# Last down-projection chunk of a decoder step by token thirds, with the final norm of a third beside the next third and two thirds scaled on GpSimd

## The chip, the core and the metric

The kernel runs on one core of a Trainium2 chip. The metric is the device time of one execution in microseconds (us), lower is better. Five engines work side by side, each through its own queue of instructions in order: TensorE (PE), VectorE (DVE), ScalarE (ACT), GpSimd (POOL) and SyncE (SP), which here only issues DMAs. They wait for one another through semaphores.

## The reference, cut to what matters

One step of a decoder layer for 1024 prompt tokens and 8 sample tokens, 1032 in all, in a model of width 1024. Only its end matters here: the feed-forward block (ConvFFN, 2816 hidden features) and the final norm.

```python
def conv_ffn(hn, buf, w_up, conv_w, conv_b, w_down):
    ...
    a, gt = jnp.split(conv, 2, axis=-1)
    return (a * jax.nn.silu(gt)) @ w_down, full[:, T:]
...
        x = x + f
...
    y = rmsnorm(x, P['norm_final'])

def rmsnorm(x, g):
    r = lax.rsqrt(jnp.mean(x * x, axis=-1, keepdims=True) + EPS)
    return (x * r) * g
```

## The kernel before

Activations lie with the 128 features of a tile on the partitions and the 1032 tokens along a row. There are KT = 8 feature tiles; XR[:, m, :] is the residual stream x of tile m. A product of a weight tile with 1032 tokens runs as NTG = 3 matmuls of TG = 344 tokens, each into its own PSUM bank. Every float32 product is made of three float32r products, of the rounded operands and the remainders: WH with HH, WH with HL, WL with HH (L256, L257, L259). ScalarE rounds a weight slab to WH (L245, `act_hi`), VectorE subtracts to get WL (L250, `dve_lo`), and both use two slots in turn. `acc(slot)` is a group of three banks: banks 0 to 2 and 3 to 5. TensorE fills a group and raises `acc_ready`; the engine that empties it raises `acc_free[slot]`.

The hidden features come in 11 chunks of 256. A loop makes a chunk of the up projection (4 groups) and then the down projection of the chunk before (8 groups, one for each m, k = 2 weight tiles each, so 18 matmuls a group). VectorE adds each group to XR (L2400). After the loop `down(0, N_SLABS - 2, ...)` does the last chunk's down projection. It needs the last two weight slabs: the four m of slab N_SLABS - 2 first, then the four of slab N_SLABS - 1. For each m, VectorE adds the group to XR (L2429), ScalarE squares the new XR tile into TMP (L390), and VectorE adds the squares to SS (L399; SS is the tile GT).

Then comes the final norm, once for all 1032 tokens. `pe_norm` sums SS over the partitions by 9 matmuls with a column of ones (L415), so that a token stands on a partition. ScalarE takes the root (L428). VectorE inverts it (L444) and spreads it onto diagonals in SS (L446, L448; `dve_norm_diag`). TensorE multiplies a matrix of ones with SS (L421), which brings the scale of each token to all partitions, and ScalarE copies it to RB (L432). VectorE scales the eight tiles of XR by RB and by the gain in one scalar_tensor_tensor each (L2434, in place), and SyncE stores each tile once it is there (L2440, `sp_final`). GpSimd does nothing in this stretch; its last instruction is the DMA of `up_state` (L2252).

For a norm in the middle of the kernel (`pe_entry`) the same steps run in between other matmuls: L1931 is the sum over partitions, L1937 the spreading. Early in the kernel GpSimd prepares tables, with tensor_tensor in lines L660 and L741 and L780, and tensor_scalar with a per-partition scalar from SBUF in L711 to L713.

Of the kernel before, what the change touches and what calls it, by code (L numbers as in the profile page):

```python
# [30 lines left out]
ACT = mybir.ActivationFunctionType  # L31
# [3 lines left out]
D = 1024  # L35
# [99 lines left out]
def program(nc, I, O):  # L135
    ctx = ExitStack()
    with ctx:
        def sem(name):
            return ctx.enter_context(nc.semaphore(name))
# [246 lines left out]
        def act_square(act, done, count, tile, slot, width):  # L386

            if done is not None:
                act.wait_ge(norm_dve, done)
            nc.scalar.activation(TMP[:, slot, 0:width], tile, ACT.Square).then_inc(sq_ready, 1)  # L390
# [1801 lines left out]
        def dve_cross(dve, st):  # L2192
# [18 lines left out]
            for t in range(8):  # L2211
                if t == MID + 2:
# [29 lines left out]
        ffn_in, u_slots, f_conv, f_silu, f_mul, f_hi, f_lo = (sem("ffn_in"), sem("u_slots"), sem("f_conv"),  # L2242
                                                               sem("f_silu"), sem("f_mul"), sem("f_hi"), sem("f_lo"))
        y_ready, y_stored, f_stored = sem("y_ready"), sem("y_stored"), sem("f_stored")

        def pool_ffn(pool):
            pool.wait_ge(acc_ready, G_CO + KT)
            pool.dma_start(FW[:], I["ffn_w"]).then_inc(ffn_in, 16)
            pool.dma_start(FB[:], I["ffn_buf"]).then_inc(ffn_in, 16)
            pool.dma_start(O["buf1"], I["buf1"]).then_inc(f_stored, 16)  # L2250
            pool.wait_ge(u_slots, 2 * NF + 2)
            pool.dma_start(O["up_state"], UPS[:]).then_inc(f_stored, 16)  # L2252
            pool.wait_ge(f_stored, 32)
            pool.wait_ge(mem_kv_out, 32)
            pool.wait_ge(s5_stored, 16)
            pool.wait_ge(ml_out, 160)
            pool.wait_ge(gl_out, 64)

        def pe_ffn(pe):
            def up(i, n, g, per_n, per_g, first=0):  # L2260
                for k in range(first, 4):
                    pe.wait_ge(w_lo, i * per_n + (n + k + 1))
                    pe.wait_ge(acc_free[(g + k) % 2], i * (per_g // 2) + (g + k) // 2)
                    split_product(pe, banks((g + k) % 2), (n + k) % 2, next_hi_cols, next_lo_cols, 0, KT).then_inc(acc_ready, 1)

            def down(i, n, g, buf, h_need, per_n, per_g, per_h):
                pe.wait_ge(f_lo, i * per_h + h_need)
                for s in range(2):
                    pe.wait_ge(w_lo, i * per_n + (n + s + 1))
                    for m in range(4):  # L2270
                        gg = g + 4 * s + m
                        pe.wait_ge(acc_free[gg % 2], i * (per_g // 2) + gg // 2)
                        split_product(pe, banks(gg % 2), (n + s) % 2,
                                      lambda k, t: HH[:, buf, k, t * TG:(t + 1) * TG],
                                      lambda k, t: HL[:, buf, k, t * TG:(t + 1) * TG],
                                      m, 2, 4).then_inc(acc_ready, 1)

            pe_entry(pe, SL_FFN, G_FFN, 3, 5)
            up(0, SL_FFN, G_FFN, 0, 0, 2)
            with pe.Fori(0, (NF // 2 - 1) // 2) as i:  # L2280
                for c in range(2):
                    n, g = SL_FFN + 4 + 6 * c, G_FFN + 4 + 12 * c
                    up(i, n, g, 12, 24)
                    down(i, n + 4, g + 4, c, 2 * c + 2, 12, 24, 4)
            down(0, N_SLABS - 2, G_FFN + 124, 0, NF, 0, 0, 0)

            pe_norm(pe, 4, N, G_FFN + 132)

        def act_ffn(act, st):
            act_entry(act, 3)  # L2290
# [27 lines left out]
            with act.Fori(0, (NF // 2 - 1) // 2) as i:  # L2318
                for c in range(2):
                    n, g = SL_FFN + 4 + 6 * c, G_FFN + 4 + 12 * c  # L2320
                    up(i, n, g, 4 + 4 * c, (c + 1) % 2, 12, 24, 8, False)
                    down(i, n + 4, g + 4, 4 + 4 * c, (c + 1) % 2, 12, 24, 8)
            for m in range(KT):
                g = G_FFN + 124 + m
                act.wait_ge(acc_free[g % 2], g // 2 + 1)
                act_square(act, 36 + m - 1, None, XR[:, m, :], m % 2, N)
            act_norm(act, 4, 6, N)

        def dve_ffn(dve, st):
            L = st.link  # L2330
# [86 lines left out]
            with dve.Fori(0, (NF // 2 - 1) // 2) as i:  # L2417
# [3 lines left out]
                    up(i, n, g, 4 + 4 * c, 2 + 2 * c, (c + 1) % 2, 12, 24, 8, False)  # L2421
                    down(i, n + 4, g + 4, 4 + 4 * c, 2 + 2 * c, (c + 1) % 2, 12, 24, 8)
                st.leave((NF // 2 - 1) // 2)
            L(nc.vector.memset(SS[:, :], 0.0))
            for m in range(KT):
                g = G_FFN + 124 + m
                dve.wait_ge(acc_ready, g + 1)
                x = XR[:, m, :]
                nc.vector.tensor_tensor(t3(x), t3(x), acc(g % 2), AD).then_inc(acc_free[g % 2], 1)  # L2429
                dve_sum(dve, KT * 4 + m, False, m % 2, N, 36 + m)  # L2430

            dve_norm_diag(dve, st, 4, N)
            for kt in range(KT):
                nc.vector.scalar_tensor_tensor(out=XR[:, kt, :], in0=XR[:, kt, :], scalar=GAIN[:, 4, kt:kt + 1],  # L2434
                                               in1=RB[:, :], op0=M, op1=M).then_inc(y_ready, 1)

        def sp_final(sp):
            for kt in range(KT):
                sp.wait_ge(y_ready, kt + 1)
                sp.dma_start(O["y"][:, kt, :], XR[:, kt, :]).then_inc(y_stored, 16)  # L2440
            sp.wait_ge(y_stored, 16 * KT)

        @block.sync
        def _(sp):
# [4 lines left out]
        def _(pool):  # L2449
# [9 lines left out]
            pool_gla(pool)  # L2459
            pool_gates(pool)  # L2460
            pool_cross(pool)
            pool_ffn(pool)

        @block.scalar
        def _(act):
# [215 lines left out]
```

## Time and profile before

| | us |
|---|---|
| median of 3 runs | 2369.13 (2362.12 to 2372.32) |
| profiled execution, its own time | 2369.92 |
| its span, first to last instruction | 2367.3 |
| PE busy in the span | 2260.8 |
| DVE busy | 1145.2 |
| ACT busy | 597.0 |
| POOL busy | 281.7 |

The span is what the views of the profile show; the execution's own time is 2.6 us longer. Busy times are sums over an engine's instructions. Line numbers such as L2429 are those of the code printed above. In the names of the profile `ps` is PSUM, and `out<-in` stands for the tile written and the tiles read.

### The profile page before, as it was taken

What the parts mean: (1) busy time and instruction counts of PE and PEld (TensorE: products, weight loads), DVE (VectorE), ACT (ScalarE), POOL (GpSimd) and SP (SyncE); (2) the same over time, 40 slices, a digit from 0 to 9 for tenths busy, and PEclk for the clock granted to TensorE, in tenths of its full rate; (3) what the DMA queues carried; (4) which work ended last, traced back from release to release, by engine and by line L of the source; (5) the groups of instructions that cost most, each with busy time, mean ns of one, the idle gap of its engine ahead of it and who ended that gap; (6) DMA issues with size and microseconds to landing.
All of it is one profiled execution on the core that took longest, in us unless ns stands there. A gap on an engine that the chain in (4) does not pass through costs nothing.

```text
span 2367.3 us, 34371 instructions
## 1 busy us (share of the span) xinstructions
PE 2260.8 (95%) x14712; PEld 2177.6 (92%) x14712; DVE 1145.2 (48%) x1264; ACT 597.0 (25%) x740; POOL 281.7 (12%) x436
## 2 busy tenths in 40 slices
PE   5799989999999999999999999999999999999995
PEld 5699978888989999999999998999999999999995
DVE  4716533334444344323654222437566655556665
ACT  4422233222322222233332124222111111111112
POOL 5989700000000000000000000000000000000000
PEclk9899999999989999999999999999999999999998
DMA  6311123121322222224322143111111111111111
GB/s 234 107 45 48 51 92 109 55 72 73 126 101 82 79 77 88 105 81 191 134 99 88 45 169 143 36 46 54 45 46 48 51 46 45 46 45 46 54 40 72
DMA packets 45221, 190.36 MB, mean 80 GB/s; under 512 B 5136, under 2 KB 5200, under 8 KB 41488
## 3 DMA queue, kind: packets, MB, share of 16 engines
q1 hardware_dynamic: 32112, 117.13, 14.4%
q0 software_dynamic: 11104, 54.41, 6.1%
q10 hardware_dynamic: 1872, 16.83, 1.8%
q8 instruction: 111, 1.82, 0.3%
q14 instruction: 22, 0.18, 0.0%
HBM read 152.59 MB, written 35.93 MB: 80 GB/s over the span
## 4 chain that ended last, share of the span: by engine, by line
PE 88%; issue 4%; DVE 3%; ACT 2%; POOL 1%; DMA 1%; DVEq 0%; ACTq 0%; POOLq 0%
PE ps L256 24%; PE ps L257 24%; PE ps L259 24%; PE ps L1715 1%; PE ps L1006 1%; PE ps L2043 1%; PE ps L2067 1%; DVE GT L399 1%; PE ps L371 1%; PE ps L372 1%; PE ps L374 1%; PE ps L2077 1%; POOL W L660 1%; PE ps L1691 0%; DVE WL L250 0%
## 5 line engine op out<-in xcount | busy, mean ns | idle before, releaser
L256 PE MATMUL ps<-XH,WH 128*128 128x344 f32 x1656 | 536.5, 327 | 8.5 <-DVE WL L250 6.0
L257 PE MATMUL ps<-XL,WH 128*128 128x344 f32 x1512 | 481.4, 322 | 0.0
L256 PE MATMUL ps<-XN,WH 128*128 128x344 f32 x1248 | 399.2, 322 | 4.3 <-issue 4.1
L257 PE MATMUL ps<-XN,WH 128*128 128x344 f32 x1248 | 397.2, 322 | 0.0
L250 DVE TENSOR_TENSOR WL<-WRAW,WH 128x1024 fp32r<-128x1024 f32 x175 | 220.3, 1260 | 309.3 <-ACT WH L245 308.2
L259 PE MATMUL ps<-XH,WL 128*128 128x344 f32 x1656 | 353.2, 322 | 0.0
L256 PEld LDWEIGHTS ps<-XH,WH 128*128 128x128 f32 x1656 | 314.8, 190 | 19.7 <-issue 14.4
L245 ACT ACTIVATE WH<-WRAW 128x1024 fp32r<-128x1024 f32 x175 | 184.3, 1054 | 534.6 <-PE ps L259 522.5
L257 PEld LDWEIGHTS ps<-XL,WH 128*128 128x128 f32 x1512 | 286.8, 190 | 0.2
L259 PEld LDWEIGHTS ps<-XH,WL 128*128 128x128 f32 x1656 | 279.4, 190 | 0.0
L259 PE MATMUL ps<-XN,WL 128*128 128x344 f32 x1248 | 264.3, 320 | 0.0
L256 PEld LDWEIGHTS ps<-XN,WH 128*128 128x128 f32 x1248 | 235.0, 188 | 6.4 <-issue 6.2
L257 PEld LDWEIGHTS ps<-XN,WH 128*128 128x128 f32 x1248 | 234.9, 188 | 0.5 <-issue 0.5
L259 PEld LDWEIGHTS ps<-XN,WL 128*128 128x128 f32 x1248 | 209.3, 188 | 0.0
L256 PE MATMUL ps<-HH,WH 128*128 128x344 f32 x528 | 167.7, 321 | 1.6 <-DVE XR L2429 1.6
L257 PE MATMUL ps<-HL,WH 128*128 128x344 f32 x528 | 167.1, 320 | 0.0
L2382 DVE TENSOR_TENSOR UB<-ps,RB 128x1032 f32<-128x1032 f32 x44 | 54.3, 1233 | 179.2 <-PE ps L259 173.5
L2400 DVE TENSOR_TENSOR XR<-XR,ps 128x1032 f32<-128x1032 f32 x80 | 98.2, 1228 | 34.5 <-PE ps L259 34.5
L311 ACT ACTIVATE STAGE<-ps 128x1032 f32<-128x1032 f32 x40 | 41.2, 1030 | 290.1 <-PE ps L259 290.1
L259 PE MATMUL ps<-HH,WL 128*128 128x344 f32 x528 | 111.9, 320 | 0.0
L256 PEld LDWEIGHTS ps<-HH,WH 128*128 128x128 f32 x528 | 99.5, 188 | 2.8 <-DVE XR L2429 2.0
L257 PEld LDWEIGHTS ps<-HL,WH 128*128 128x128 f32 x528 | 99.4, 188 | 0.0
(512 smaller groups left out, 3165.9 us busy)
## 6 DMA issues: line engine op xcount, KB each, us to landing
WRAW<-in_wslabs SPq DMA_DIRECT2D x175, 512.0 KB, 3.5
scratch_spill<-STAGE SPq DMA_DIRECT2D x40, 516.0 KB, 2.6
ZS<-scratch_spill POOLq DMA_DIRECT2D x24, 516.0 KB, 5.5
XIN<-in_xT POOLq DMA_DIRECT2D x1, 4128.0 KB, 18.4
XR<-in_xT ACTq DMA_DIRECT2D x2, 2064.0 KB, 8.7
out_y<-XR SPq DMA_DIRECT2D x8, 516.0 KB, 3.0
CACHES<-in_ck ACTq DMA_DIRECT2D x4, 1024.0 KB, 14.2
CACHES<-in_cv ACTq DMA_DIRECT2D x4, 1024.0 KB, 15.6
```

What stands on the lines that cost most here:

```text
L245: nc.scalar.activation(WH[:, slot], WRAW[:, slot], ACT.Copy).then_inc(w_hi, 1)
L250: nc.vector.tensor_tensor(WL[:, slot], WRAW[:, slot], WH[:, slot].bitcast(F32), ALU.subtract).then_inc(w_lo, 1)
L256: pe.matmul(out[t], WH[:, slot, w, :], xh(k, t), start=(k == 0), stop=False)
L257: pe.matmul(out[t], WH[:, slot, w, :], xl(k, t), start=False, stop=False)
L259: last = pe.matmul(out[t], WL[:, slot, w, :], xh(k, t), start=False, stop=(k == nk - 1))
L311: nc.scalar.activation(t3(staged(g)), acc(0), ACT.Copy, scale=FILL_SCALE[g]).then_inc(fl_free, 1)
L371: pe.matmul(out[t], WH[:, slot, k, :], xh_cols(k, t), start=(k == 0), stop=False)
L372: pe.matmul(out[t], WH[:, slot, k, :], xl(k, t), start=False, stop=False)
L374: last = pe.matmul(out[t], WL[:, slot, k, :], xh_cols(k, t), start=False, stop=(k == KT - 1))
L399: nc.vector.tensor_tensor(SS[:, 0:width], SS[:, 0:width], TMP[:, slot, 0:width], ALU.add).then_inc(norm_dve, 1)
L2382: nc.vector.tensor_tensor(t3(UB[:, k % 2, 2:N + 2]), acc((g + k) % 2), t3(RB[:, :]), M).then_inc(acc_free[(g + k) % 2], 1)
L2400: nc.vector.tensor_tensor(t3(x), t3(x), acc(gg % 2), AD).then_inc(acc_free[gg % 2], 1)
```

## The change

The last chunk's down projection runs over thirds of the tokens on the outside and over m on the inside. A group is then one m of one third: six matmuls into one bank, `ps[:, i % 6, 0:TG]`, with i = 8t + m from 0 to 23. Six banks are used in turn. TensorE waits for both last slabs (`w_lo >= N_SLABS`) before the first group.

VectorE adds a group to a third of XR (`add`), ScalarE squares it into one of four small tiles SQ, VectorE adds it to the third of SS (`total`; for m = 0 a copy, so the memset goes). The norm of third t - 1 runs between the groups of third t: the sums over partitions after its group m = 3 (`pe_end_columns`, 3 columns), root and diagonals (`act_end_root`, `dve_end_diag`), the spreading after group m = 5 (`pe_end_spread`), and the copy to RB (`act_end_rows`). The last third's norm follows its last group.

GpSimd scales the first two thirds (`pool_end`): for each m a tensor_scalar with the gain and then a tensor_tensor with RB, in place on 344 tokens, the second waiting for the first; 32 instructions. VectorE scales the last third, one instruction for each m. SyncE stores six pieces in place of eight, each of four tiles m of one third, in the order of the thirds; rows of 344 tokens (1376 bytes) in place of 1032 tokens.

The diff, without the parts that only pass arguments:

```diff
@@ -2242,14 +2242,26 @@
         ffn_in, u_slots, f_conv, f_silu, f_mul, f_hi, f_lo = (sem("ffn_in"), sem("u_slots"), sem("f_conv"),
                                                                sem("f_silu"), sem("f_mul"), sem("f_hi"), sem("f_lo"))
         y_ready, y_stored, f_stored = sem("y_ready"), sem("y_stored"), sem("f_stored")
-
-        def pool_ffn(pool):
+        end_added, G_END = acc_free[0], G_FFN + 124
+        ADDED = (G_END + 1) // 2
+        SQ = at("SQ", [128, 4, TG], O_TMP)
+
+        def third(t):
+
+            return slice(t * TG, t * TG + TG)
+
+        def end_bank(i):
+
+            return ps[:, i % 6, 0:TG]
+
+        def pool_ffn(pool, st):
             pool.wait_ge(acc_ready, G_CO + KT)
             pool.dma_start(FW[:], I["ffn_w"]).then_inc(ffn_in, 16)
             pool.dma_start(FB[:], I["ffn_buf"]).then_inc(ffn_in, 16)
             pool.dma_start(O["buf1"], I["buf1"]).then_inc(f_stored, 16)
             pool.wait_ge(u_slots, 2 * NF + 2)
             pool.dma_start(O["up_state"], UPS[:]).then_inc(f_stored, 16)
+            pool_end(pool, st)
             pool.wait_ge(f_stored, 32)
             pool.wait_ge(mem_kv_out, 32)
             pool.wait_ge(s5_stored, 16)
@@ -2282,9 +2294,63 @@
                     n, g = SL_FFN + 4 + 6 * c, G_FFN + 4 + 12 * c
                     up(i, n, g, 12, 24)
                     down(i, n + 4, g + 4, c, 2 * c + 2, 12, 24, 4)
-            down(0, N_SLABS - 2, G_FFN + 124, 0, NF, 0, 0, 0)
-
-            pe_norm(pe, 4, N, G_FFN + 132)
+            pe.wait_ge(f_lo, NF)
+            pe.wait_ge(w_lo, N_SLABS)
+            for t in range(NTG):
+                for m in range(KT):
+                    i = KT * t + m
+                    if i < 6:
+                        evacuated(pe, G_END)
+                    else:
+                        pe.wait_ge(end_added, ADDED + i - 5)
+                    s = (N_SLABS - 2 + m // 4) % 2
+                    for k in range(2):
+                        w, c = m % 4 + 4 * k, third(t)
+                        pe.matmul(end_bank(i), WH[:, s, w, :], HH[:, 0, k, c], start=(k == 0), stop=False)
+                        pe.matmul(end_bank(i), WH[:, s, w, :], HL[:, 0, k, c], start=False, stop=False)
+                        last = pe.matmul(end_bank(i), WL[:, s, w, :], HH[:, 0, k, c], start=False, stop=(k == 1))
+                    last.then_inc(acc_ready, 1)
+                    if t and m == 3:
+                        pe_end_columns(pe, t - 1)
+                    if t and m == 5:
+                        pe_end_spread(pe, t - 1)
+            pe_end_columns(pe, NTG - 1)
+            pe_end_spread(pe, NTG - 1)
+
+        def pe_end_columns(pe, t):
+
+            pe.wait_ge(norm_dve, 36 + KT * t + KT)
+            if t:
+                pe.wait_ge(norm_act, 8 + 2 * t)
+            for j, first in enumerate((0, 128, TG - 128)):
+                last = pe.matmul(ps[:, 6, j:j + 1], SS[:, t * TG + first:t * TG + first + 128], ONES[:, 0:1],
+                                 start=True, stop=True)
+            last.then_inc(norm_pe, 1)
+
+        def pe_end_spread(pe, t):
+
+            pe.wait_ge(norm_tail, 2 + t + 1)
+            pe.matmul(ps[:, 7, 0:TG], ONES, SS[:, third(t)], start=True, stop=True).then_inc(norm_pe, 1)
+
+        def act_end_root(act, t):
+
+            act.wait_ge(norm_pe, 8 + 2 * t + 1)
+            nc.scalar.activation(NRM[:, 0:3], ps[:, 6, 0:3], ACT.Sqrt, bias=EPSC, scale=1.0 / D).then_inc(norm_act, 1)
+
+        def act_end_rows(act, t):
+
+            act.wait_ge(norm_pe, 8 + 2 * t + 2)
+            nc.scalar.activation(RB[:, third(t)], ps[:, 7, 0:TG], ACT.Copy).then_inc(norm_act, 1)
+
+        def dve_end_diag(dve, st, t):
+
+            dve.wait_ge(norm_act, 8 + 2 * t + 1)
+            st.link(nc.vector.reciprocal(NRM[:, 0:3], NRM[:, 0:3]))
+            c = t * TG
+            st.link(nc.vector.tensor_scalar(SS[:, c + 256:c + TG], IDENT[:, 384 - TG:128], NRM[:, 2:3], None, ALU.mult))
+            nc.vector.tensor_tensor(SS[:, c:c + 256].rearrange("p (c i) -> p c i", i=128),
+                                    IDENT.unsqueeze(1).to_broadcast([128, 2, 128]),
+                                    NRM[:, 0:2].unsqueeze(2).to_broadcast([128, 2, 128]), ALU.mult).then_inc(norm_tail, 1)
 
         def act_ffn(act, st):
             act_entry(act, 3)
@@ -2320,11 +2386,19 @@
                     n, g = SL_FFN + 4 + 6 * c, G_FFN + 4 + 12 * c
                     up(i, n, g, 4 + 4 * c, (c + 1) % 2, 12, 24, 8, False)
                     down(i, n + 4, g + 4, 4 + 4 * c, (c + 1) % 2, 12, 24, 8)
-            for m in range(KT):
-                g = G_FFN + 124 + m
-                act.wait_ge(acc_free[g % 2], g // 2 + 1)
-                act_square(act, 36 + m - 1, None, XR[:, m, :], m % 2, N)
-            act_norm(act, 4, 6, N)
+            for t in range(NTG):
+                for m in range(KT):
+                    i = KT * t + m
+                    act.wait_ge(end_added, ADDED + i + 1)
+                    if i >= 4:
+                        act.wait_ge(norm_dve, 36 + i - 3)
+                    nc.scalar.activation(SQ[:, i % 4, :], XR[:, m, third(t)], ACT.Square).then_inc(sq_ready, 1)
+                    if t and m == 3:
+                        act_end_root(act, t - 1)
+                    if t and m == 5:
+                        act_end_rows(act, t - 1)
+            act_end_root(act, NTG - 1)
+            act_end_rows(act, NTG - 1)
 
         def dve_ffn(dve, st):
             L = st.link
@@ -2421,24 +2495,54 @@
                     up(i, n, g, 4 + 4 * c, 2 + 2 * c, (c + 1) % 2, 12, 24, 8, False)
                     down(i, n + 4, g + 4, 4 + 4 * c, 2 + 2 * c, (c + 1) % 2, 12, 24, 8)
                 st.leave((NF // 2 - 1) // 2)
-            L(nc.vector.memset(SS[:, :], 0.0))
+            dve.wait_ge(norm_rb, 2)
+
+            def add(i):
+                t, m = divmod(i, KT)
+                dve.wait_ge(acc_ready, G_END + i + 1)
+                x = XR[:, m, third(t)]
+                nc.vector.tensor_tensor(x, x, end_bank(i), AD).then_inc(end_added, 1)
+
+            def total(i):
+                t, m = divmod(i, KT)
+                dve.wait_ge(sq_ready, KT * 4 + i + 1)
+                if m == 0:
+                    nc.vector.tensor_copy(SS[:, third(t)], SQ[:, i % 4, :]).then_inc(norm_dve, 1)
+                else:
+                    dve.wait_ge(norm_dve, 36 + i)
+                    nc.vector.tensor_tensor(SS[:, third(t)], SS[:, third(t)], SQ[:, i % 4, :], AD).then_inc(norm_dve, 1)
+
+            for i in range(KT * NTG):
+                add(i)
+                if i:
+                    total(i - 1)
+                if i >= KT and i % KT == 3:
+                    dve_end_diag(dve, st, i // KT - 1)
+            total(KT * NTG - 1)
+            dve_end_diag(dve, st, NTG - 1)
+            dve.wait_ge(norm_act, 8 + 2 * NTG)
             for m in range(KT):
-                g = G_FFN + 124 + m
-                dve.wait_ge(acc_ready, g + 1)
-                x = XR[:, m, :]
-                nc.vector.tensor_tensor(t3(x), t3(x), acc(g % 2), AD).then_inc(acc_free[g % 2], 1)
-                dve_sum(dve, KT * 4 + m, False, m % 2, N, 36 + m)
-
-            dve_norm_diag(dve, st, 4, N)
-            for kt in range(KT):
-                nc.vector.scalar_tensor_tensor(out=XR[:, kt, :], in0=XR[:, kt, :], scalar=GAIN[:, 4, kt:kt + 1],
-                                               in1=RB[:, :], op0=M, op1=M).then_inc(y_ready, 1)
+                x = XR[:, m, third(NTG - 1)]
+                nc.vector.scalar_tensor_tensor(out=x, in0=x, scalar=GAIN[:, 4, m:m + 1], in1=RB[:, third(NTG - 1)],
+                                               op0=M, op1=M).then_inc(xn_ready, 1)
+
+        def pool_end(pool, st):
+            for t in range(NTG - 1):
+                pool.wait_ge(norm_act, 8 + 2 * t + 2)
+                for m in range(KT):
+                    x = XR[:, m, third(t)]
+                    st.link(nc.gpsimd.tensor_scalar(x, x, GAIN[:, 4, m:m + 1], None, ALU.mult))
+                    nc.gpsimd.tensor_tensor(x, x, RB[:, third(t)], ALU.mult).then_inc(y_ready, 1)
 
         def sp_final(sp):
-            for kt in range(KT):
-                sp.wait_ge(y_ready, kt + 1)
-                sp.dma_start(O["y"][:, kt, :], XR[:, kt, :]).then_inc(y_stored, 16)
-            sp.wait_ge(y_stored, 16 * KT)
+            for t in range(NTG):
+                for k in range(2):
+                    if t < NTG - 1:
+                        sp.wait_ge(y_ready, KT * t + 4 * k + 4)
+                    else:
+                        sp.wait_ge(xn_ready, KT * 2 + 4 * k + 4)
+                    sp.dma_start(O["y"][:, 4 * k:4 * k + 4, third(t)], XR[:, 4 * k:4 * k + 4, third(t)]).then_inc(y_stored, 16)
+            sp.wait_ge(y_stored, 16 * 2 * NTG)
 
         @block.sync
         def _(sp):
```

## Rows read from the trace of the kernel before

**Rows 1.** The page: busy us (share of the span) and instructions of each engine.

```profile
PE 2260.8 (95%) x14712; PEld 2177.6 (92%) x14712; DVE 1145.2 (48%) x1264; ACT 597.0 (25%) x740; POOL 281.7 (12%) x436
```

**Rows 2.** Chain that ended last, 2311 us on: start us, us, what.

```profile
2314.82 1.24 DVE XR L2429
2316.08 1.07 ACT TMP L390
2317.18 1.23 DVE GT L399
...
2349.10 0.14 issue
2349.24 3.49 PE ps L421 x6
```

**Rows 3.** Timeline of TensorE, 2311 to 2314 us: start us, us.

```profile
2311.11 0.32 PE L256 MATMUL ps<-HH,WH 128*128 128x344 f32 x1
...
2313.95 0.32 PE L256 MATMUL ps<-HH,WH 128*128 128x344 f32 x1
```

**Rows 4.** Timeline of VectorE, last weight slab and final norm.

```profile
2312.48 1.23 DVE L250 TENSOR_TENSOR WL<-WRAW,WH 128x1024 fp32r<-128x1024 f32 x1
...
2347.60 0.23 DVE L446 TENSOR_SCALAR GT<-CF,NRM 128x8 f32<-128x8 f32 x1
2347.87 1.23 DVE L448 TENSOR_TENSOR GT<-CF,NRM 128x1024 f32<-128x1024 f32 x1
2353.82 9.72 DVE L2434 SCALAR_TENSOR_TENSOR XR<-XR,SC,RB 128x1032 f32<-128x1032 f32 x8 [4.73 <-ACT RB L432]
```

**Rows 5.** The stores: DMA issues by line, then the stretch in which they run.

```profile
out_y<-XR SPq DMA_DIRECT2D x8, 516.0 KB, 3.0
...
2356.00:2363.00 7.00, 0.00 (x0) 0.00 (x0) 7.00 (x7) 0.00 (x0) 0.00 (x0) 0.50 1.01 408
```

**Rows 6.** Groups by line and shape, and L1931 and L1937 by themselves.

```profile
L428 ACT ACT_TABLE_LOAD x3 | 3.8, 1283 | 0.1
L390 ACT ACTIVATE TMP<-MEMT 128x256 f32<-128x256 f32 x8 | 3.2, 415 | 6.8 <-DMA MEMT<-in_memT 6.2
L466 DVE TENSOR_TENSOR MEML<-TMP,MEMH 128x256 fp32r<-128x256 f32 x8 | 3.4, 420 | 0.3 <-ACT MEMH L439 0.2
L1931 PE MATMUL ps<-CF,GT 128*128 128x1 f32 x32 | 3.7, 245 | 0.0
L1937 PE MATMUL ps<-GT,CF 128*128 128x512 f32 x8 | 3.8, 592 | 0.0
```

**Rows 7.** Timeline of GpSimd, 130 to 137 us, VectorE idle.

```profile
130.30 0.74 POOL L741 TENSOR_TENSOR RC<-SCR 128x256 f32<-128x256 f32 x1
...
135.58 1.30 POOL L741 TENSOR_TENSOR RC<-SCR 128x512 f32<-128x512 f32 x1
```

**Rows 8.** Timelines of VectorE and then GpSimd, 62 to 77 us.

```profile
62.72 1.28 DVE L399 TENSOR_TENSOR GT<-GT,TMP 128x1032 f32<-128x1032 f32 x1
...
67.47 1.43 DVE L250 TENSOR_TENSOR WL<-WRAW,WH 128x1024 fp32r<-128x1024 f32 x1
...
74.50 2.32 DVE L250 TENSOR_TENSOR WL<-WRAW,WH 128x1024 fp32r<-128x1024 f32 x1
...
63.01 2.42 POOL L711 TENSOR_SCALAR SB<-SB,SC 128x512 f32<-128x512 f32 x1
65.53 3.17 POOL L712 TENSOR_SCALAR SCC<-SCC,SC 128x512 f32<-128x512 f32 x1
68.79 0.93 POOL L713 TENSOR_SCALAR H<-H,SC 128x256 f32<-128x256 f32 x1
...
73.57 2.17 POOL L660 TENSOR_TENSOR BB<-BB,SCR 128x512 f32<-128x512 f32 x1
```

**Rows 9.** Timelines of VectorE and then GpSimd, 267 to 269 us.

```profile
267.05 1.23 DVE L856 TENSOR_TENSOR T<-ps,RC 128x1024 f32<-128x1024 f32 x1 [12.74 <-PE ps L949]
...
267.10 1.17 POOL L741 TENSOR_TENSOR OT<-SCC,PW 128x576 f32<-128x576 f32 x1
```

More of the change, by code:

```diff
@@ L2461, in _ @@
             pool_cross(pool)
-            pool_ffn(pool)
+            pool_ffn(pool, st)
         @block.scalar
```

## Prediction

> **What bounds the kernel now.** I read the page first. TensorE is busy for 95% of the span [rows 1], so outside the end the matmuls set the time, and the change doesn't touch them. What is left to win lies where TensorE waits, and that is the last 54 us. I read that stretch in the chain that ended last, then engine by engine in the timelines.
>
> In the loop over the eight m the chain doesn't run over TensorE but round a ring: VectorE adds (L2429), ScalarE squares (L390), VectorE sums (L399). From one L2429 to the next it is 1.24 + 1.07 + 1.15 and some gaps, about 3.5 us [rows 2], while a group of 18 matmuls takes 2.84 us (2311.11 to 2313.95) [rows 3]. Behind the loop everything is serial: sums over partitions, root, diagonals, spreading from 2349.24 to 2352.7 [rows 2], copy, eight scalings from 2353.82 to 2363.54 [rows 4], and 3.8 us until the last piece is stored, at 2367.3. TensorE is down to half its clock by then: one of the six spreading instructions takes 3.49 / 6 = 0.58 us for 344 columns [rows 2], where L1937 between other matmuls takes 3.8 / 8 = 0.475 for 512 [rows 6]. The change attacks all of this: the ring shortens, two thirds of the norm lie beside matmuls, and the scaling is shared. The question is whether the engine that takes the scaling can carry it.
>
> **The new start.** The outermost loop is the tokens now, so the first third needs both slabs. WL of the last one is done at 2312.48 + 1.23 = 2313.71 [rows 4]. From such an end to the next matmul it is 0.14 us [rows 2], so TensorE starts at 2313.85 and not at 2311.11 [rows 3]: 2.7 us lost. Nothing covers them; TensorE has nothing else to do there.
>
> **TensorE's groups.** 24 groups of 6 matmuls each, 2.84 / 3 = 0.945 us [rows 3]. The count of matmuls stays 144. VectorE per group: from the 256-column tensor_tensor (0.42 us) and the 1032-column one (1.23) I get 0.51 for 344 columns, of which 0.08 overlap with the next (1.15 against 1.23) [rows 2, 4, 6]. That is 0.43 to 0.5 for the add and the same for the sum, 0.86 to 1.0 in all: about TensorE's own pace. ScalarE's square is 0.49, between 0.415 at 256 and 1.07 at 1032 [rows 2, 6]. So third 0 takes 8 x 0.945 and the ring of before is gone.
>
> **Norm of third 0 beside third 1.** Group 11 (m = 3) has been issued by 2313.85 + 12 x 0.945 = 2325.19, with its result about 0.2 later. VectorE adds until 2325.9, ScalarE squares until 2326.4. Then comes the table load for the root, 1.28 us [rows 6], so until 2327.7, and the root, 0.3, until 2328.0. I count the load once: before, squares follow Silu and the copy to RB follows the root without one. A square after a root isn't shown there; a load for it would start GpSimd 1.3 us later, none of it a gain, and I take none. TensorE's three columns (6 instructions at 3.7 / 32 = 0.12 [rows 6], 0.7 us) lie beside that. VectorE has been standing in front of the reciprocal since about 2326.4 with the adds of groups 12 and 13 queued behind it. The diagonals (reciprocal and tail 0.52, from 2347.35 to 2347.87, and 0.42 for 256 columns [rows 4, 6]) end at 2329.0. TensorE has done two groups by 2327.8 and waits until 2329.15: 1.3 us lost. Spreading is two passes of 344 columns, by the 0.475 for 512, 0.64 us, results at 2330.1. ScalarE has two squares in front of the copy to RB and ends it at 2331.3. **GpSimd starts at about 2331.35**, TensorE starts third 2 at 2331.7.
>
> **GpSimd's 32 instructions.** This is where the sum is decided. Tensor_tensor of plain rows takes 0.74 us for 256 columns and 1.30 for 512 with VectorE idle [rows 7]; 344 columns give 0.93. Of tensor_scalar with a scalar from SBUF no clean row exists. L711 (512 columns) lasts from 63.01 to 65.43, but until 64.0 VectorE's L399 runs, and what remains is 1.43; L713 (256 columns) lasts from 68.79 to 69.72, and L250 runs until 68.90: 0.82 remain [rows 8]. A line through 0.82 and 1.43 gives 1.03 at 344; with some of the preparation hidden in the blocked part I take 1.08. Bounds: below, 0.55, if the remainders hold a wait that isn't plain (first rival); above, L711 as it stands, 2.42 for 512, hence 1.6. I stay with the remainders, because in [rows 8] the blocking is plain. With 0.08 after each for the wait for its semaphore (L711 ends at 65.43, L712 starts at 65.53, and L712 and L713 alike) a pair costs 2.16, 16 pairs 34.6 us. Alone, GpSimd ends at 2366.0, 1.3 us before the old kernel's span ends with its stores.
>
> **Contention.** When GpSimd's and VectorE's instructions both read two SBUF operands, they take turns: L250 at 74.50 lasts 2.32 in place of 1.23 beside the GpSimd instruction at 73.57, which itself takes 2.17 in place of 1.30 [rows 8]. Where one of VectorE's operands is in PSUM, there is nothing: 1.23 for VectorE and 1.17 for GpSimd [rows 9]. So the adds pass freely, and the sums (10 of them after 2331), parts of two norms (2 instructions each) and the 8 scalings of the last third collide: 22 instructions of some 0.45, 10 us if each held GpSimd up for its whole length. A tensor_scalar lets VectorE in early, though: L250 at 67.47 lost only 0.2 us beside L712. About half the collisions are then free for GpSimd; I take 5.5 us, between 3 and 10. GpSimd ends at 2366.0 + 5.5 = 2371.5.
>
> The Trainium skill (SBUF, "Who interferes with whom") says the pair of ports is an exclusive lock, held for the whole instruction. The alternation in the rows agrees, the 0.2 us do not. By the rule all 10 us would count, and the sum would be 4.5 us higher.
>
> VectorE itself: a sum waits up to 0.9 us for a tensor_tensor on GpSimd, so a group costs it 1.25 in place of 0.95. Third 2 then ends around 2346.5, the last norm (columns, root, diagonals, spreading, copy, some on a cold TensorE) around 2352, the scalings around 2360. That is 11 us before GpSimd is through, so all of this hides behind GpSimd, and so do the 2.7 and 1.3 us of TensorE.
>
> **The stores.** SyncE's queue is in order of the thirds. The second piece of third 1 waits for GpSimd's last instruction, and both pieces of third 2, ready long before, are queued behind it. So at the end three DMAs of 704 KB (together 2.11 MB) start together: at 408 GB/s 5.2 us, and a fixed part of 3.0 - 1.3 = 1.7 from a 516 KB piece that lands in 3.0 [rows 5]; with issue and end 7.4 us. Before, it was 3.8 us. The rows of 1376 bytes appear nowhere in this trace; nothing to 2 us for them, I take 0. End of the span 2371.5 + 7.4 = 2378.9, against 2367.3. The execution's own time lies 2.6 above the span: 2381.5. The profiled execution of before had 2369.92, the median is 2369.13, so no correction between them beyond 0.8. **I predict 2382 us**, 12 to 13 us or 0.5% slower.
>
> **Rivals.** (1) Cheap tensor_scalar, not slower. If one SBUF input needs only about half the time per column, a tensor_scalar of 344 is 0.55, and GpSimd is 16 x 0.53 = 8.5 us earlier: 2373.5. For it: the remainders in [rows 8] could hold a wait that the timeline doesn't show. Against it: two lengths fit one line. It decides from 0.98 us a piece downwards: then the sum is 1.6 us less, under 2380. The Trainium skill (GPSIMD Engine Reference, "Engine selection") says that one-input work on GpSimd runs at roughly line rate, which is this rival; by its 1.2 GHz, 344 columns would be an estimated 0.3 us plus the start, and the sum as in this rival or 3 us below it. The 1.43 us for 512 speak against it. Chance 0.17.
>
> (2) Full lock: every one of VectorE's 22 collisions holds GpSimd for its whole length, or tensor_scalar waits twice, for its scalar and for its tile (L712 waited past two of VectorE's). 5 to 8 us more: 2388. Chance 0.20.
>
> (3) GpSimd keeps up and VectorE's chain sets the end. Third 2 would end at 2340.6, the last norm's copy at about 2346, eight scalings of 0.43 at 2349.4, one DMA 3.8 us: span 2353.2, time 2356, faster by 13 us. It needs 32 instructions in 18 us, 0.56 each, and 0.93 is measured for every second. Chance 0.03.
>
> **How the numbers follow.** My forecast, GpSimd sets the end with 1.08 and half the collisions, has 0.60 and spans 2377 to 2386. A measurement of this kernel tells 0.5% (11.8 us) from no change, so slower begins at 2381. Of the 0.60, 0.36 lie above that and 0.24 below. Slower: 0.36 + 0.19 of rival 2 = 0.55. Within 0.5%: 0.24 + 0.01 + 0.16 of rival 1 = 0.41. Faster: 0.04. Range 2372 to 2391.
>
> **What would show it.** GpSimd busy almost without a gap from 2331 to 2371, with tensor_scalar around 1.1 and tensor_tensor at 0.93 alone and more beside VectorE; its last instruction about 10 us after VectorE's; the last three stores issued together. TensorE's first group at 2313.85; a wait of 1.3 us in front of the first spreading. Wrong would be: a tensor_scalar under 0.9 us, sums on VectorE that don't stretch beyond 0.6 us beside GpSimd, or a last store that waits on VectorE.

## The result and the profile after

The changed kernel takes 2378.73 us (median of 20 runs) against 2371.44 us. The ratio is 1.0039 with a 95% interval of 1.0029 to 1.0049, so it is about 9 us slower, between 7 and 12. (The medians alone are 7.3 us apart. The ratio rests on all twenty runs of each kernel, which scatter over 12 and 13 us; their means are 9.0 us apart.) I had forecast 2382 us, 12 to 13 us slower, within a range of 2372 to 2391. The direction and the cause are as forecast. The size is a fourth smaller, and so it falls just within the 0.5% that I had given 0.41, and not into the 0.55 above it.

The page of the changed kernel, beside which [rows 1] are read:

```profile
span 2381.2 us, 34489 instructions
## 1 busy us (share of the span) xinstructions
PE 2261.8 (95%) x14712; PEld 2178.1 (91%) x14712; DVE 1145.3 (48%) x1301; ACT 601.0 (25%) x760; POOL 318.6 (13%) x468
...
out_y<-XR SPq DMA_DIRECT2D x6, 688.0 KB, 3.4
```

TensorE's work is the same to 1 us. GpSimd has 37 us more. The span is 14 us longer, but part of that isn't the change: the last weight slab's subtraction (L250), up to which the code is the same, starts at 2316.48 here and at 2312.48 before [rows 4]. Over all the executions profiled below this start lies between 2306.6 and 2316.5. I therefore count every trace from the start of that instruction to the end of the span. Before it is 2367.3 - 2312.48 = 54.8 us, after the change 2381.2 - 2316.48 = 64.7 us: 9.9 us, which agrees with the 9.2 us of the ratio.

What follows is the chain that ended last in the changed kernel (start us, us, what), where [rows 2] had VectorE, ScalarE and TensorE in turn:

```profile
2316.48 1.24 DVE WL L250
2317.72 0.09 issue
2317.81 0.40 PE ps L2309
...
2332.04 1.28 ACT L2338
2333.32 0.01 issue
2333.33 0.27 ACT NRM L2338
...
2336.28 0.44 ACT RB L2343
2336.72 0.10 issue
2336.82 1.52 POOL XR L2534
2338.34 0.07 issue
2338.41 0.93 POOL XR L2535
...
2371.32 1.12 POOL XR L2534
2372.44 0.04 issue
2372.48 0.04 POOLq L2268
2372.52 0.91 POOL XR L2535
```

L2309 is the first matmul of a group by thirds, L2338 the root with its table load, L2343 the copy to RB, L2534 GpSimd's tensor_scalar and L2535 its tensor_tensor. From 2336.82 to 2373.43 every step of the chain is GpSimd. VectorE is through with its own scalings at 2360.0:

```profile
2353.90 6.10 DVE L2526 SCALAR_TENSOR_TENSOR XR<-XR,SC,RB 128x344 f32<-128x344 f32 x8 [2.10 <-ACT RB L2343]
```

So the last 13 us of GpSimd's list have nothing beside them but stores. Parts of the timelines, VectorE's and then GpSimd's, beside which [rows 7 to 9] are read:

```profile
2338.77 0.94 DVE L2513 TENSOR_TENSOR GT<-GT,SQ 128x344 f32<-128x344 f32 x1
...
2340.72 0.50 DVE L2513 TENSOR_TENSOR GT<-GT,SQ 128x344 f32<-128x344 f32 x1
...
2345.11 0.51 DVE L2513 TENSOR_TENSOR GT<-GT,SQ 128x344 f32<-128x344 f32 x1
...
2345.96 1.19 DVE L2513 TENSOR_TENSOR GT<-GT,SQ 128x344 f32<-128x344 f32 x1
```

```profile
2338.41 0.93 POOL L2535 TENSOR_TENSOR XR<-XR,RB 128x344 f32<-128x344 f32 x1
2339.32 1.41 POOL L2534 TENSOR_SCALAR XR<-XR,SC 128x344 f32<-128x344 f32 x1
2340.81 1.20 POOL L2535 TENSOR_TENSOR XR<-XR,RB 128x344 f32<-128x344 f32 x1
...
2344.37 1.41 POOL L2534 TENSOR_SCALAR XR<-XR,SC 128x344 f32<-128x344 f32 x1
2345.86 0.92 POOL L2535 TENSOR_TENSOR XR<-XR,RB 128x344 f32<-128x344 f32 x1
...
2364.96 1.14 POOL L2534 TENSOR_SCALAR XR<-XR,SC 128x344 f32<-128x344 f32 x1
2366.19 0.91 POOL L2535 TENSOR_TENSOR XR<-XR,RB 128x344 f32<-128x344 f32 x1
2367.07 1.14 POOL L2534 TENSOR_SCALAR XR<-XR,SC 128x344 f32<-128x344 f32 x1
```

Alone (the last rows) a pair takes 2.11 us from start to start: 1.14 for the tensor_scalar, 0.91 for the tensor_tensor. Beside VectorE a tensor_scalar mostly becomes 1.41 (1.51 at most, the first one in the chain above) and a tensor_tensor 1.20 at most. What a sum of VectorE (L2513) loses depends on what GpSimd is in the middle of. The sums at 2338.77 and 2345.96 come after the start of a tensor_tensor and become 0.94 and 1.19. The sum at 2340.72 starts 0.09 us before one; it keeps its 0.50, and the tensor_tensor takes 1.20. The sum at 2345.11 lies wholly within the tensor_scalar at 2344.37, and it keeps its 0.51 too.

Something that I hadn't in the sum stands at the start. These are stretches of the changed kernel (us, then busy time of PE, PEld, DVE, ACT, POOL, the granted clock, DMA share, GB/s):

```profile
2315.00:2317.80 2.80, 0.28 (x2) 0.02 (x1) 2.39 (x2) 1.06 (x1) 0.00 (x0) 1.00 0.01 3
2317.80:2319.00 1.20, 1.19 (x7) 1.20 (x8) 0.00 (x0) 0.00 (x0) 0.00 (x0) 0.94 0.00 0
2319.00:2322.30 3.30, 3.30 (x14) 3.30 (x13) 1.28 (x3) 0.98 (x2) 0.00 (x0) 0.50 0.02 5
2322.30:2330.00 7.70, 7.70 (x51) 7.70 (x50) 7.34 (x16) 3.83 (x8) 0.00 (x0) 1.00 0.00 1
```

TensorE waits 2.5 us for the last slab, resumes at the full 2.4 GHz, and 1.2 us later runs at 1.2 GHz for 3.3 us. In that time a matmul follows the one before every 0.29 us in place of 0.16, which costs 1.5 us.

### The profile page after: what moved, and what is told of

It reads as the page before. It is cut to its first block, busy times and chain, and to the rows that moved or that the text cites. A ratio compares the mean times of both kernels' runs of the same rounds, so it can differ in the third digit from the quotient of the medians.

```text
span 2381.2 us, 34489 instructions
## 1 busy us (share of the span) xinstructions
PE 2261.8 (95%) x14712; PEld 2178.1 (91%) x14712; DVE 1145.3 (48%) x1301; ACT 601.0 (25%) x760; POOL 318.6 (13%) x468
## 4 chain that ended last, share of the span: by engine, by line
PE 88%; issue 4%; POOL 3%; DVE 2%; ACT 2%; DMA 1%; DVEq 0%; ACTq 0%; POOLq 0%
PE ps L256 24%; PE ps L257 24%; PE ps L259 23%; PE ps L1715 1%; PE ps L1006 1%; PE ps L2043 1%; PE ps L2067 1%; POOL XR L2534 1%; PE ps L371 1%; POOL XR L2535 1%; PE ps L372 1%; PE ps L374 1%; PE ps L2077 1%; POOL W L660 1%; DVE WL L250 1%
## 5 line engine op out<-in xcount | busy, mean ns | idle before, releaser
L250 DVE TENSOR_TENSOR WL<-WRAW,WH 128x1024 fp32r<-128x1024 f32 x175 | 222.5, 1272 | 309.0 <-ACT WH L245 308.1
L256 PE MATMUL ps<-HH,WH 128*128 128x344 f32 x480 | 151.9, 319 | 0.0
L257 PE MATMUL ps<-HL,WH 128*128 128x344 f32 x480 | 151.8, 320 | 0.0
L259 PE MATMUL ps<-HH,WL 128*128 128x344 f32 x480 | 101.7, 320 | 0.0
L256 PEld LDWEIGHTS ps<-HH,WH 128*128 128x128 f32 x480 | 90.3, 188 | 0.0
```

Source lines behind the costliest of these rows:

```text
L250: nc.vector.tensor_tensor(WL[:, slot], WRAW[:, slot], WH[:, slot].bitcast(F32), ALU.subtract).then_inc(w_lo, 1)
L256: pe.matmul(out[t], WH[:, slot, w, :], xh(k, t), start=(k == 0), stop=False)
L257: pe.matmul(out[t], WH[:, slot, w, :], xl(k, t), start=False, stop=False)
L259: last = pe.matmul(out[t], WL[:, slot, w, :], xh(k, t), start=False, stop=(k == nk - 1))
```

## The experiments

The verdicts are read from the ratio to the kernel before on the same chip. Behind them stand the times from the start of the last L250 in the profiled execution (before: 54.8 us, changed: 64.7 us). The changed kernel has 20 runs, the others 5 to 12 each, on three chips. "Under the changed kernel" is therefore a difference of two such distances from the kernel before.

| run | ratio (95%) | us against before | L250 to end |
|---|---|---|---|
| changed kernel | 1.0039 (1.0029 to 1.0049) | +9.2 | 64.7 |
| VectorE scales all | 0.9976 (0.9965 to 0.9987) | -5.7 | 49.2 |
| GpSimd one third | 0.9978 (0.9967 to 0.9988) | -5.2 | 51.6 |
| early first groups | 1.0026 (1.0015 to 1.0037) | +6.2 | 60.3 |
| stores reordered | 1.0037 (1.0024 to 1.0050) | +8.8 | 62.6 |
| no gain on GpSimd | 0.9965 (0.9951 to 0.9979) | -8.3 | 48.5 |
| gain early | 0.9978 (0.9968 to 0.9987) | -5.2 | 50.6 |
| before with one GpSimd instruction | 1.0021 (1.0012 to 1.0030) | +5.0 | 59.1 |
| early start and split | 0.9954 (0.9941 to 0.9968) | -10.9 | 43.6 |
| early start, no GpSimd | 0.9962 (0.9949 to 0.9976) | -9.0 | 43.5 |
| split again | 0.9950 (0.9937 to 0.9964) | -11.8 | 43.7 |

**VectorE scales all.** This tells the theory (GpSimd's list sets the end) from the rival that the order by thirds itself costs the time.

```diff
-            dve.wait_ge(norm_act, 8 + 2 * NTG)
-            for m in range(KT):
...
-        def pool_end(pool, st):
-            for t in range(NTG - 1):
-                pool.wait_ge(norm_act, 8 + 2 * t + 2)
+            for t in range(NTG):
+                dve.wait_ge(norm_act, 8 + 2 * t + 2)
...
+        def pool_end(pool, st):
+            pass
```

> GpSimd scales nothing; VectorE scales all three thirds after the last diagonals, 24 instructions in place of 8. Theory A (GpSimd's 32 instructions set the end of the changed kernel): GpSimd's 36.6 us fall away, VectorE's chain sets the end: diagonals done some 33.5 us after the last weight slab, 24 x 0.43 = 10.3 us, one store 3.8 us. That is 17 us under the changed kernel and about 8 us (0.3%) under the kernel before. Theory B (the order by thirds and the norms between the groups cost the time, GpSimd is cover): VectorE has 7 us more work and nothing is won, 9 to 16 us over the kernel before.

15 us under the changed kernel and 5.7 us under the kernel before. The rest of the change, without GpSimd, is a gain. Expected were 8 us; the timeline of VectorE has most of the difference:

```profile
2349.22 0.43 DVE L2351 TENSOR_TENSOR GT<-CF,NRM 128x256 f32<-128x256 f32 x1
2349.56 11.78 DVE L2527 SCALAR_TENSOR_TENSOR XR<-XR,SC,RB 128x344 f32<-128x344 f32 x24
```

The diagonals end 33.5 us after L250, as expected, but a scaling takes 11.78 / 24 = 0.49 us and not 0.43, which makes 1.5 us for the 24.

**GpSimd has one third.**

```diff
+            for t in (1, 2):
...
-            for t in range(NTG - 1):
+            for t in range(1):
                 pool.wait_ge(norm_act, 8 + 2 * t + 2)
```

> GpSimd scales third 0 only (16 instructions), VectorE thirds 1 and 2. Theory A: GpSimd is done 20 us after its start, about when VectorE has done 12 of its 16; VectorE's chain sets the end with up to 2 us from collisions: 15 us under the changed kernel, 6 us under the kernel before. Theory B: as the changed kernel or slower, 9 us or more over the kernel before.

5.2 us under the kernel before, where 6 were expected, and no difference from VectorE alone. With half of its list GpSimd is no longer the end (its last instruction ends at 2354.0, VectorE's at 2359.2), but its help is eaten. VectorE's 16 scalings take 9.77 us, 0.61 each, beside it, and they begin 35.3 us after L250, where VectorE alone begins at 33.4; so both kernels are through with scaling 45 us after L250. Then come 6.6 us to the end in place of 4.1. The second store of third 0 waits for GpSimd until 2354.0, the four others come behind it in SyncE's queue, and data then moves without a break from about 2355 to 2365. In this profiled execution the stores set the end.

**Early first groups.**

```diff
-            return ps[:, i % 6, 0:TG]
+            return ps[:, (i + 3) % 6, 0:TG]
...
-            pe.wait_ge(w_lo, N_SLABS)
+            pe.wait_ge(w_lo, N_SLABS - 1)
...
+                    if i == 4:
+                        pe.wait_ge(w_lo, N_SLABS)
-                    if i < 6:
-                        evacuated(pe, G_END)
+                    if i < 3:
+                        pe.wait_ge(acc_free[1], G_END // 2)
+                    elif i < 6:
+                        pe.wait_ge(end_added, ADDED)
```

> The first four groups of third 0 wait only for the slab that they use, and the six banks begin with the three that are free first; TensorE doesn't stop before them. Everything else as in the changed kernel. Theory A: all behind it moves forward by the 2.5 us wait, and if the fall of TensorE's clock to 0.5 for 3.3 us came from that wait, by 1.6 us more: 4.1 us under the changed kernel, 5 us over the kernel before. If the clock falls all the same: 2.5 us. Rival: GpSimd's start doesn't hang on it, 0 us.

6.2 us over the kernel before, where 5 were expected; counted from L250 4.4 us under the changed kernel. The granted clock stays at 1.00 in every one of the 14 us after the last slab. I looked at the same microseconds in the other runs with thirds. Of the six profiled executions with the wait (the changed kernel, VectorE alone, one third, reordered stores, no gain, gain early) five fall to 0.50 for some 3.3 us. Of the four without it (this one, the two with the split and the one without GpSimd), none does. The wait brings the fall, then, but not every time. The same is seen once more further on. Where TensorE waits 2.2 to 2.5 us before the first spreading (gain early and both executions of the split), the clock falls to 0.50 within 1.1 us of its start and stays there for 3.3 us; where it waits 1.1 us (the other seven), it doesn't fall there.

**Stores reordered.**

```diff
-            for t in range(NTG):
-                for k in range(2):
+            for t, k in ((0, 0), (0, 1), (2, 0), (2, 1), (1, 0), (1, 1)):
```

> SyncE stores third 2 before third 1, otherwise the changed kernel. Theory A (GpSimd's last instruction releases the end, and two stores that were ready are queued behind it): only one store of 688 KB comes after GpSimd's last instruction, 3.8 to 4.2 us in place of 7.8: 3.6 to 4 us under the changed kernel, 5.5 us over the kernel before. Rival (the last stores take as long one by one): under 1 us.

No difference that can be told from the changed kernel, 1.0037 against 1.0039. (From L250 on it is 2.1 us less, but 1.5 of these are there when GpSimd ends: this is the one execution with the wait in which the clock didn't fall.) Both sides of the expectation had the mechanism wrong. The transfers do end earlier. These are SyncE's waits at the end and then the last stretches of this run:

```profile
SPq L137 <- PEq L137: 3.5, 1, 3.5
SPq L137 <- DMA out_y<-XR: 3.0, 1, 3.0
```

```profile
2368.50:2370.50 2.00, 0.00 (x0) 0.00 (x0) 0.00 (x0) 0.00 (x0) 0.00 (x0) 0.50 0.89 329
2371.00:2374.50 3.50, 0.00 (x0) 0.00 (x0) 0.00 (x0) 0.00 (x0) 0.00 (x0) 0.50 0.00 0
```

The last store has landed by 2370.9, and then nothing moves for 3.5 us, while SyncE stands in its last wait, at the end of the program (L137). In the changed kernel that wait is 0.2 us and the wait for the store 5.2. The view names PE's queue, but TensorE has been done for long. GpSimd's last instruction ended at 2367.42, 7.1 us before the end.

**One GpSimd instruction in the kernel before.** So I put one at the end of the old kernel, which nobody waits for.

```diff
             pool.dma_start(O["up_state"], UPS[:]).then_inc(f_stored, 16)
+            pool.wait_ge(y_ready, KT)
+            nc.gpsimd.tensor_tensor(TMP[:, 0, 0:TG], TMP[:, 1, 0:TG], RB[:, 0:TG], ALU.mult)
```

> The kernel before, and after VectorE's last scaling one tensor_tensor of 344 columns on GpSimd that nobody waits for. If GpSimd's queue needs 7.1 us from its last arithmetic instruction to the end, whatever the stores do, the end is at 1.0 + 7.1 after the last scaling in place of 3.8: 4.3 us over the kernel before. If the 3.5 us without any transfer at the end of the run with reordered stores come from the stores: 0 us.

1.0021, 5.0 us; and 59.1 - 54.8 = 4.3 us from L250 on, to the tenth what was expected. GpSimd's timeline, and SyncE's waits:

```profile
2365.10 0.90 POOL L2254 TENSOR_TENSOR TMP<-TMP,RB 128x344 f32<-128x344 f32 x1 [62.34 <-DVE XR L2436]
```

```profile
SPq L137 <- PEq L137: 4.5, 1, 4.5
SPq L137 <- DMA out_y<-XR: 3.0, 1, 3.0
```

The instruction ends at 2366.00, the span at 2373.1: again 7.1 us.

**No gain on GpSimd.** This leaves the gain of the final norm out for the first two thirds, and so half of GpSimd's list.

```diff
-                    st.link(nc.gpsimd.tensor_scalar(x, x, GAIN[:, 4, m:m + 1], None, ALU.mult))
```

> Leaves the gain of the first two thirds out: GpSimd has 16 tensor_tensor in place of 32 instructions. Theory A (the length of GpSimd's list sets the end): 16 x 1.22 us fall away, GpSimd is done about 39 us after the last weight slab, and now VectorE's last scaling and its store, or the 7.1 us that follow GpSimd's last instruction in the run with the stores reordered, end the kernel: 18 us under the changed kernel, 9 us under the kernel before. Theory C (what costs is that GpSimd takes part at all: taking turns with VectorE, and the 7 us behind its last instruction): most of it stays, less than 10 us under the changed kernel.

8.3 us under the kernel before, 9 expected. That GpSimd takes part is not what made the changed kernel slow; the length of its list behind the scale is. Taking part isn't free, though: VectorE starts the last diagonals 37.0 us after L250 here, at 32.5 in the run with VectorE alone. GpSimd's last instruction ends at 2351.9, 5 us before VectorE's (2357.3), whose store then ends the kernel.

**Gain early.** All 32 instructions stay, but the 16 gains don't wait for the norm.

```diff
         def pool_end(pool, st):
+            for i in range(KT * (NTG - 1)):
+                t, m = divmod(i, KT)
+                x = XR[:, m, third(t)]
+                pool.wait_ge(sq_ready, KT * 4 + i + 1)
+                nc.gpsimd.tensor_scalar(x, x, GAIN[:, 4, m:m + 1], None, ALU.mult).then_inc(end_gain, 1)
             for t in range(NTG - 1):
                 pool.wait_ge(norm_act, 8 + 2 * t + 2)
...
-                    st.link(nc.gpsimd.tensor_scalar(x, x, GAIN[:, 4, m:m + 1], None, ALU.mult))
+                    pool.wait_ge(end_gain, 2 + KT * t + m + 1)
```

> GpSimd's 32 instructions all stay, but each gain comes as soon as ScalarE has squared the piece, 16 us before the scale of its third is there. Theory A (its list sets the end because it starts late): the list starts 15 us earlier, GpSimd is through about 43 us after the last weight slab, plus 7.1 us: 15 us under the changed kernel, 6 us under the kernel before. Theory C: more collisions with VectorE's sums in thirds 0 and 1 slow the whole chain, less than 8 us under the changed kernel.

5.2 us under the kernel before, where 6 were expected, with the same work on the same engine:

```profile
2310.51 1.15 POOL L2535 TENSOR_SCALAR XR<-XR,SC 128x344 f32<-128x344 f32 x1 [15.09 <-ACT SQ L2396]
...
2332.49 16.43 POOL L2541 TENSOR_TENSOR XR<-XR,RB 128x344 f32<-128x344 f32 x16
```

GpSimd is through 42.3 us after L250, 43 expected. What ends this kernel is VectorE: its last scaling ends 46.8 us after L250, 3.3 later than in the changed kernel, because its sums and last diagonals wait for one tensor_tensor after another and TensorE's clock falls a second time. A store of 3.8 us follows. The rival had a true part, then, but a small one.

**Early start and split.** The version that the runs so far point to. The early start is that of "Early first groups". GpSimd has third 0 alone, its gains early. VectorE scales three pieces of third 1 while it waits for the root of the last third, five behind the diagonals, and then third 2.

```diff
+            scale(1, range(0, 3))
             dve_end_diag(dve, st, NTG - 1)
+            scale(1, range(3, KT))
+            scale(2, range(KT))
```

> Early first groups; GpSimd only third 0, its gains early; VectorE third 1 in the waits of the last norm, then third 2. Theory A: GpSimd is done long before the end, 4.1 us from the early start, VectorE's last scaling 41.5 us after the last weight slab less 4.1, and a store of 3.7: 19 to 20 us under the changed kernel, 10 to 11 us under the kernel before. Theory C: collisions eat half of that, 5 us under the kernel before.

0.9954, 10.9 us faster than the kernel before, as expected (10 to 11), and 43.6 us from L250 on against 54.8. GpSimd is done at 2340.2 and VectorE at 2353.7, without a gap behind the last diagonals:

```profile
2316.27 9.14 POOL L2542 TENSOR_SCALAR XR<-XR,SC 128x344 f32<-128x344 f32 x8 [13.47 <-ACT SQ L2400]
2331.56 8.60 POOL L2547 TENSOR_TENSOR XR<-XR,RB 128x344 f32<-128x344 f32 x8 [6.16 <-ACT RB L2348]
```

```profile
2347.32 6.42 DVE L2530 SCALAR_TENSOR_TENSOR XR<-XR,SC,RB 128x344 f32<-128x344 f32 x13
```

**The same without GpSimd, and the split again.** Is GpSimd worth anything when it isn't in the way?

```diff
-            scale(1, range(0, 3))
+            scale(0, range(0, 3))
             dve_end_diag(dve, st, NTG - 1)
-            scale(1, range(3, KT))
+            scale(0, range(3, KT))
+            scale(1, range(KT))
             scale(2, range(KT))
```

> As the run with the early start and the split, but VectorE scales all three thirds (three pieces before the last diagonals, 21 behind them) and GpSimd does nothing. What is GpSimd's help worth when it is not in the way? From the two traces with VectorE alone and with the split: the last diagonals come 2.5 us earlier without collisions, but 8 more scalings of 0.49 follow: 1.5 us slower than the split, 9.5 us under the kernel before. If the collisions cost as much as the help gives: no difference.

> The early start and the split once more, on the same chip as the run without GpSimd, so that the two can be compared: 10 to 11 us under the kernel before, 1.5 us under the run without GpSimd.

9.0 us without and 11.8 us with GpSimd under the kernel before. The two intervals overlap, and from L250 on the profiled executions have 43.5 and 43.7 us. VectorE's last diagonals and scalings, without GpSimd and then with it, show why so little is left:

```profile
2342.34 0.17 DVE L2352 RECIPROCAL NRM<-NRM 128x3 f32<-128x3 f32 x1
...
2343.19 10.32 DVE L2529 SCALAR_TENSOR_TENSOR XR<-XR,SC,RB 128x344 f32<-128x344 f32 x21
```

```profile
2344.55 0.17 DVE L2353 RECIPROCAL NRM<-NRM 128x3 f32<-128x3 f32 x1
...
2345.39 6.42 DVE L2530 SCALAR_TENSOR_TENSOR XR<-XR,SC,RB 128x344 f32<-128x344 f32 x13
```

GpSimd takes 8 scalings off VectorE, 3.9 us. But counted from L250 the last diagonals begin at 32.5 us with GpSimd and at 28.4 without, 4.1 us later, where 2.5 were expected. Beside the gains VectorE's sums take up to 0.78 in place of 0.51, TensorE then waits 2.4 us before the first spreading in place of 1.1, and its clock falls. Whether the split is worth the 1.5 us expected stays open; in the profiled executions it is worth nothing from L250 on. That GpSimd can be left out of the end altogether at no more than a few us is shown.

## Why the prediction was right, and where its sizes were off

All times here count from the start of L250, the forecast ones from 2312.48.

**The new start.** TensorE's first group was put at 1.37 and is at 1.33. The wait was put at 2.7 us and is 2.5; that it takes the clock with it was missing from the sum. Group 11 came 1.6 us later than forecast, nearly all of it for that reason, and so did all that hangs on it.

**The norm beside the next third.** Forecast: diagonals at 16.5, GpSimd's start at 18.9. Measured: 18.1 and 20.3. In the run with reordered stores, where the clock didn't fall, GpSimd starts at 18.8. The table load came once. TensorE waited 1.1 us before the first spreading, 1.3 forecast.

**GpSimd's own length.** 16 pairs of 2.16, 34.6 us; measured 2.11, 33.8 us. The tensor_scalar that had to be read out of blocked rows was put at 1.08 and is 1.14. The 0.08 us that I added behind each instruction are there behind the tensor_scalar and not behind the tensor_tensor (2366.19 + 0.91 is past the next start, 2367.07), so two small errors nearly cancel in the pair. This was the term that decided, and the remainders in [rows 8] were the right way to it. What I held against the first rival, that two lengths fit one line, was no evidence: two points always do. The first rival, a tensor_scalar of 0.55, is out: one SBUF input is no cheaper on GpSimd here than two (1.14 against 0.91 alone). The rule of the Trainium skill (GPSIMD Engine Reference, "Engine selection") that one-input work runs at roughly line rate isn't what these rows show.

**Contention.** This is the step whose size was furthest off: 5.5 us forecast, within 3 to 10, and 36.6 - 33.8 = 2.8 us measured. I had counted about half of 22 collisions at a whole VectorE instruction, 0.45 us. GpSimd's timeline has ten lengthened instructions, eight tensor_scalar and two tensor_tensor, and they lose 0.17 to 0.37 us each: the count was about right, the price too high by more than half. When a tensor_tensor is under way it is VectorE's sum that waits, 0.3 to 0.7 us, and the eight scalings take 6.10 us in place of 3.9. The second rival, a lock that holds GpSimd up for every instruction, is out with it. The forecast that a tensor_scalar lets VectorE through early held (the sum at 2345.11). Third 2 ended near 2348.6, 32 us from L250 (34 forecast).

**The stores.** 7.4 us forecast and 7.8 measured, but for a reason half of which I didn't know. Two limits lie within a us of each other. The three stores have landed 7.6 us after GpSimd's last instruction (the 7.8 less SyncE's last wait of 0.2), and in the two runs where the stores don't set the end, it comes 7.1 us after that instruction. The forecast price of the queued stores was right; what it implied, that another order would give 3.6 us back, was wrong, as the reordered run shows.

**The sum.** 18.9 + 34.6 + 5.5 + 7.4 = 66.4 forecast; 20.3 + 33.8 + 2.8 + 7.8 = 64.7 measured. The errors are +1.4, -0.8, -2.7 and +0.4. They partly cancel, and that 1.7 us is left and not more is in part luck. Most of the rest of the distance between the forecast 12 to 13 us and the measured 9 isn't in the terms: the sum itself gives 66.4 - 54.8 = 11.6 us, and I had rounded 2381.5 up to 2382 and set it against a median 0.8 us below the profiled execution. The third rival, that GpSimd keeps up, is out: it would have needed 0.56 an instruction, and 1.06 is the mean of the pair alone.

**Where the gain went.** The order by thirds and the norms beside matmuls (no run tells the two apart) are worth 5.7 us as they stand, and 9 to 12 with the early start and three scalings moved into a wait. The changed kernel gave this back, and 9 us more, by putting 36.6 us of work behind the first scale, on an engine that had stood idle until then.

## What to carry to other kernels

Before work moves to an idle engine, multiply its count by that engine's price and lay it from its first possible start to the end: here 32 x 1.06 us from a point 20 us behind the last slab could not fit into the 54.8 us of before. Ask next which part of the work can start before its last input: the gains alone, moved 16 us forward, turned 9 us slower into 5 us faster. Charge the help with what it takes from the helped engine: in the split, GpSimd took 3.9 us of scalings off VectorE and made its chain 4.1 us longer. A wait on TensorE costs more than its length when the clock falls after it (2.5 us and 1.5 more here), so start the first groups on what is already there.

## What the runs showed of the hardware that I had not expected

- Where the last arithmetic instruction on GpSimd comes near the end, the span ends 7.1 us after it, though the stores have landed and nothing waits for it: 7.1 us in the run with reordered stores, 7.1 us in the old kernel with one instruction added (4.3 us from L250 on, 5.0 by the ratio). What GpSimd does in that time no row shows.
- After a wait of 2.5 us TensorE ran 0.8 to 1.4 us at 2.4 GHz (1.1 to 1.2 in the changed kernel) and then some 3.3 us at 1.2 GHz, in five of six executions; without the wait, in four, it didn't. The three executions with a wait of 2.2 to 2.5 us before the first spreading show the same fall, the seven with 1.1 us there don't.
- When GpSimd and VectorE take turns, the loss is unequal here: VectorE's sums of 0.50 us became up to 1.19, GpSimd's instructions lost some 0.3. The Trainium skill (SBUF — State Buffer, "Who interferes with whom") has whoever issues first hold the shared ports for the whole instruction. For the tensor_tensor the rows agree. For the tensor_scalar they don't: VectorE's sum from 2345.11 to 2345.62 ran at its full pace inside the tensor_scalar that lasted from 2344.37 to 2345.78.
